# The second layer's modulation as one block behind the first layer's last projection, with early loads

## The reference, cut to what matters

```python
def hybrid_layer(x, c, pos0, k_buf, v_buf, shift_prev, wkv0, conv_buf, h0, lp):
    mod = jax.nn.silu(c) @ lp["w_mod"] + lp["b_mod"]          # (., 3072)
    shift_m, scale_m, gate_m = jnp.split(mod, 3, axis=-1)
    h = rmsnorm(x, lp["norm_pre"]) * (1.0 + scale_m[:, None]) + shift_m[:, None]
    proj = h @ lp["w_in"]                                     # (., 2880)
    qa, ka, va, ga, pb, gb, xc, gc = jnp.split(proj, IN_OFFSETS, axis=-1)
    ...   # A: sliding-window attention, B: RWKV-7 time mixing, C: RG-LRU, each gated
    y = jnp.concatenate([ya, yb, yc], axis=-1) @ lp["w_out"]
    x = x + gate_m[:, None] * rmsnorm(y, lp["norm_post"])
    return x, (k_new, v_new, shift_new, wkv_new, conv_new, h_new)
```

## Time and profile before

| | us |
|---|---|
| three timed runs | 2907.3, 2910.8, 2911.9 |
| the profiled execution, its own time | 2903.7 |
| its span, first to last instruction | 2901.9 |
| TensorE busy in it | 2757.8 (95%) |
| TensorE weight loads | 2016.0 (69%) |
| DVE busy | 1720.0 (59%) |
| ACT busy | 1338.5 (46%) |
| POOL busy | 255.2 (9%) |
| moved by DMA | 119.18 MB |

### The profile page before, as it was taken

The page is one execution under the profiler, slowest core; times in us unless marked ns, Lnnn a source line. Parts: engine busy times, 40 slices in busy tenths (PEclk is TensorE's granted clock), DMA queues, the critical chain, the costliest instruction groups (busy, mean ns, idle before and its releaser), DMA issues.

```text
span 2901.9 us, 63519 instructions
## 1 busy us (share of the span) xinstructions
PE 2757.8 (95%) x25044; PEld 2016.0 (69%) x25044; DVE 1720.0 (59%) x4641; ACT 1338.5 (46%) x3128; POOL 255.2 (9%) x357
## 2 busy tenths in 40 slices
PE   6999999999999999997769999999999999999976
PEld 5777777777777777775457777777777777777753
DVE  1666666666666666665416666665666666666654
ACT  1545444544554444443215544445445554444432
POOL 0010111101101011100001000111011100011000
PEclk8999999999999999999769999999999999999997
DMA  9200000000000000000660000000000000000001
GB/s 341 97 16 24 23 24 23 9 24 24 24 24 17 23 24 23 16 9 22 206 243 16 19 22 23 24 23 17 16 24 24 24 20 21 24 23 16 16 19 33
DMA packets 55176, 119.18 MB, mean 41 GB/s; under 512 B 15312, under 2 KB 27216, under 8 KB 54608
## 3 DMA queue, kind: packets, MB, share of 16 engines
q1 hardware_dynamic: 52912, 114.28, 11.5%
q10 hardware_dynamic: 1952, 0.48, 0.1%
HBM read 96.34 MB, written 18.41 MB: 40 GB/s over the span
## 4 chain that ended last, share of the span: by engine, by line
PE 91%; DVE 4%; DMA 2%; issue 1%; ACT 1%; SPq 0%; POOL 0%; DVEq 0%; POOLq 0%; ACTq 0%
PE G L468 17%; PE G L576 16%; PE M L792 15%; PE G L463 8%; PE M L463 5%; PE M L625 5%; PE M L459 4%; PE M L638 3%; PE G L693 2%; PE G L474 2%; DMA RB<-in_w_mod 2%; PE M L604 1%; PE M L674 1%; PE G L459 1%; DVE Q L1441 1%
## 5 line engine op out<-in xcount | busy, mean ns | idle before, releaser
L468 PEld LDWEIGHTS G<-hT,w_in 128*128 128x128 f32 x4224 | 495.2, 194 | 21.9 <-issue 16.5
L468 PE MATMUL G<-hT,w_in 128*128 128x128 f32 x4224 | 507.1, 278 | 3.3 <-issue 3.3
L576 PE MATMUL G<-hT,w_in 128*128 128x256 f32 (+1 forms) x2048 | 497.1, 385 | 0.0
L792 PE MATMUL M<-w_out,yT 128*128 128x512 f32 x1024 | 452.8, 596 | 5.8 <-DVE yT L1579 5.8
L576 PEld LDWEIGHTS G<-hT,w_in 128*128 128x128 f32 x2048 | 360.4, 189 | 64.7 <-issue 12.3
L792 PEld LDWEIGHTS M<-w_out,yT 128*128 128x128 f32 x1024 | 193.4, 191 | 225.2 <-issue 223.7
L463 PE MATMUL G<-w_in,hT 128*128 128x512 f32 x512 | 244.4, 610 | 0.0
L1441 DVE TENSOR_TENSOR Q<-Q,M 64x256 f32<-64x256 f32 x320 | 133.8, 418 | 130.5 <-PE M L638 127.3
L625 PEld LDWEIGHTS M<-W 64*64 64x64 f32 x4608 | 147.7, 135 | 24.3 <-issue 24.3
L625 PE MATMUL M<-W 64*64 64x64 f32 x4608 | 162.7, 219 | 0.0
L1231 POOL TENSOR_TENSOR RA<-RA,small 128x1024 f32<-128x1024 f32 x32 | 60.6, 1895 | 1136.9 <-DVE small L1493 1136.9
(11 more groups left out here) (413 smaller groups left out, 4562.7 us busy)
## 6 DMA issues: line engine op xcount, KB each, us to landing
w_in<-in_w_in SPq DMA_DIRECT2D x8, 2048.0 KB, 15.1
RA<-in_w_mod SPq DMA_DIRECT2D x16, 512.0 KB, 6.9
W<-in_w_mod SPq DMA_DIRECT2D x16, 512.0 KB, 6.9
xa<-in_x_prompt SPq DMA_DIRECT2D x16, 512.0 KB, 3.7
w_out<-in_w_out SPq DMA_DIRECT2D x2, 4096.0 KB, 18.4
G<-in_x_prompt SPq DMA_DIRECT2D x16, 512.0 KB, 3.5
x_mid<-RA SPq DMA_DIRECT2D x16, 512.0 KB, 2.9
xa<-x_mid SPq DMA_DIRECT2D x16, 512.0 KB, 3.6
```

Of the source, the lines that this page charges most:

```text
L468: last = mm(out[0:width, :], Win[:, k, col:col + width], H[:, k, :], start=k == 0, stop=k == KC - 1)
L576: last = mm(out, Win[:, k, col:col + P], moving, start=k == 0, stop=k == KC - 1)
L792: last = mm(o[:, :], yT[:, k, :], Wout[:, k, 512 * h:512 * h + 512], start=k == 0, stop=k == KC - 1)
```

## The change

- **Start.** SP loads cT first, then chunks of `w_mod`, then two constants, x of tile 0 and 1; ACT takes its silu as soon as cT is there (`c_in`) and loads the other constants itself. The parameters `prm` and `spc` hold both layers, and both layers' softplus chains run behind the first layer's modulation.
- **Second x by another buffer.** Tile 1's x goes to `x2`, which shares `KB` (KR and BK as one tile), and DVE normalises it from there into `xa`.
- **Front.** The gb fill stands ahead of `front`, with its own weight semaphore; on ACT, `decays` comes behind the gb copy.
- **Sample's input early.** The last tile of each layer holds ssq between the two halves of its projection, and DVE's `sample_input()` behind `yB_ready`.
- **Modulation of layer 2.** Its 24 chunks go to six buffers `wnext` that are idle by the end of layer 1's last tile; TensorE computes them as one block behind that tile's projection, into `M0, M1, G0, M2, M0, M1`; ACT copies rows and channels. `modulation(1)` stands in the sample's DVE list.
- **Tile 0 of layer 2** is loaded, normalised and transposed within the end of layer 1's sample.
- **State stores** go out on ACT's queue, after `o_ready` of the last tile. DVE clears the states for layer 2 (`cleared`) behind its first row copy of the sample's projection; it waits for the stores.

The diff, cut to its core:

```diff
+            sp.dma_start(cT[:, :, :], d["cT"]).then_inc(L["c_in"], 16)
             for q in range(NWM - 1):
                 load_w_mod(0, q)
+            sp.dma_start(cst[:, 0:2 * P], d["cst"][:, 0:2 * P]).then_inc(L["const"], 16)
+            sp.dma_start(qk[:, 0:384], d["masks"]).then_inc(L["const"], 16)
...
+        wnext = [flat(xa[:, :]), hT[:, :, 0, :], flat(RA[:, 0:1024]), flat(KB[:, :, :].rearrange("p a b -> p (a b)")),
+                 hT[:, :, 1, :], flat(RB[:, :])]
...
+                def load_next(q):
+                    if q >= NWM:
+                        sp.wait_ge(L["mod_mm"], 24 + (q - NWM + 1))
+                    sp.dma_start(wnext[q % NWM], d["w_mod"][1, q]).then_inc(wmod_in[q % NWM], 16)
...
+                if mixed:
+                    m = NT - 1
+                    sp.wait_ge(s["xT_hi"], DONE(m))
+                    load_next(0)
+                    sp.wait_ge(s["gbc_mm"], DONE(m - 1))
+                    load_next(1)
+                    sp.wait_ge(s["pT1_mm"], DONE(m))
+                    load_next(2)
+                    sp.wait_ge(s["y_mm"], DONE(m))
+                    sp.dma_start(xr, rows(src, m)).then_inc(L["xr_in"], 16)
+                    load_next(3)
+                    sp.wait_ge(s["gbc_mm"], DONE(m))
+                    load_next(4)
+                    sp.wait_ge(s["pv_mm"], DONE(m))
+                    load_next(5)
+                    for q in range(NWM, 24):
+                        load_next(q)
+                    sp.wait_ge(s["o_ready"], DONE(m))
+                    sp.dma_start(rows(dst, m), ob).then_inc(L["y_out"], 16)
+                    sp.wait_ge(L["mod_mm"], 48)
...
+                if mixed:
+                    load_x2(d["x_mid"][P:2 * P, :])
+                    sp.wait_ge(L["modT_mm"], 1 + MODG)
...
+                    sp.wait_ge(smp["dve"], AT("y", l))
+                    sp.dma_start(xa[:, :], d["x_mid"][0:P, :]).then_inc(L["x_in"], 16)
...
                     project(0, M5).then_inc(s["o0_mm"], 1)
                     if ahead:
                         front(n + 1)
+                    else:
+                        pe.wait_ge(smp["dve"], AT("sq", l))
+                        for k in range(KC):
+                            last = mm(M3[:, 0:B], ...)
+                        last.then_inc(smp["pe"], 1)
                     project(1, M4).then_inc(s["o1_mm"], 1)
+                    if fused:
+                        pe.wait_ge(L["padded"], 2)
+                        mod_chunks(0, 1, 2, 3, 4, 5, 6, 7)
+                        mod_fold(0)
+                        pe.wait_ge(s["gbc_out"], DONE(n))
+                        mod_chunks(8, 9, 10, 11)
+                        mod_fold(1)
...
+                        mod_chunks(20, 21, 22, 23)
+                        mod_fold(4)
+                        mod_fold(5)
...
                 for g, (col, width, _) in enumerate(DGROUPS):
+                    if mixed and g == 1:
+                        pe.wait_ge(L["mod_act"], MFOLD[5])
...
+                if mixed:
+                    x_lo((l + 1) * NT)
                 pe.wait_ge(smp["dve"], AT("osq", l))
...
+                if mixed:
+                    x_hi((l + 1) * NT)
...  (ACT)
+                act.wait_ge(s["o_ready"], DONE(l * NT + NT - 1))
+                for out, carry in ((d["k_p"], kT[:, 0:P]), (d["v_p"], Vt[:, 0, :]), (d["shift_p"], pB[:, :, 0]),
+                                   (d["wkv_p"], S[:, 0, :, :]), (d["conv_p"], xcb[:, :, 0:3]), (d["h_p"], hcar[:, :])):
+                    act.dma_start(out[l], carry, ...).then_inc(L["state"], 16)
...  (DVE)
+            def cleared(l):
                 dve.wait_ge(L["state"], l * 96 + 16)
                 ms(pB[:, :, 0:1], 0.0)
...
-                    mask = cst[upper, o:o + 2 * CH].rearrange("p (w c) -> p w c", w=2)
+                    mask = cst[upper, o:o + 3 * CH].rearrange("p (w c) -> p w c", w=3)[:, 0::2]
...
                 for g, (_, width, _) in enumerate(DGROUPS):
                     dve.wait_ge(L["row_mm"], l * (ROWS - MODG) + (g + 1))
-                    cp(rowbuf[g % 2][:, 0:width], (G0, G1)[g % 2][:, 0:width]).then_inc(L["row_out"], 1)
+                    cp(srow[g % 2][:, 0:width], (G1, G0)[g % 2][:, 0:width]).then_inc(L["row_out"], 1)
+                    if mixed and g == 0:
+                        cleared(l + 1)
...
+                if mixed:
+                    dve.wait_ge(L["mod_act"], MFOLD[5])
+                    modulation(l + 1)
```

More of the change, by code:

```diff
@@ L477, in _, with to_channels @@
             for l in range(DEPTH):
-                def to_channels(group, row, out, rows, chunks):
-                    pe.wait_ge(L["row_out"], l * ROWS + (row + 1))
+                def to_channels(buf, row, out, rows, chunks):
+                    pe.wait_ge(L["row_out"], row + 1)
                     for start, width, column in chunks:
-                        last = mm(out[0:width, column:column + rows], rowbuf[group % 2][:, start:start + width],
+                        last = mm(out[0:width, column:column + rows], buf[:, start:start + width],
                                   fold[:, 0:rows], start=True, stop=True)
@@ L774, in tile @@
                         fill_rk(n + 1, Hn)
+                    fused = mixed and not ahead
                     pe.wait_ge(s["yn_ready"], DONE(n))
@@ L827, in _ @@
                 pe.wait_ge(s["o1_mm"], BEFORE((l + 1) * NT))
-                pe.wait_ge(smp["dve"], AT("sq", l))
-                for k in range(KC):
-                    last = mm(M0[:, 0:B], one, dsq[:, k, :], start=k == 0, stop=k == KC - 1)
-                last.then_inc(smp["pe"], 1)
                 pe.wait_ge(smp["dve"], AT("h", l))
@@ L1134, in tile @@
                         low_rank(n + 1)
+                    fused = mixed and not ahead
                     act.wait_ge(s["o0_mm"], DONE(n))
-                    A(RB[:, 0:512], M5[:, :], ACT.Square, accum_out=small[:, 3:4])
+                    A(RB[:, 0:512] if ahead else stB, M5[:, :], ACT.Square, accum_out=small[:, 3:4])
                     if ahead:
                         decays(n + 1)
+                    else:
+                        act.wait_ge(smp["dve"], AT("ms", l))
+                        A(dr2[:, :], dr1[:, :], ACT.Sqrt).then_inc(smp["act"], 1)
@@ L1139, in tile @@
                     act.wait_ge(s["o1_mm"], DONE(n))
-                    A(RB[:, 512:1024], M4[:, :], ACT.Square, accum_out=small[:, 4:5]).then_inc(s["o_squared"], 1)
-                x_square(l * NT, hT[:, :, 1, :])
-                act.wait_ge(L["mod_out"], l + 1)
-                act.wait_ge(L["zeros"], l + 1)
-                h_lo(l * NT, hT[:, :, 0, :])
-                h_hi(l * NT, hT[:, :, 0, :])
-                for step in (copy_rk, copy_wka, copy_v, low_rank, decays):
+                    A(RB[:, 512:1024] if ahead else qk[:, 0:512], M4[:, :], ACT.Square, accum_out=small[:, 4:5]).then_inc(s["o_squared"], 1)
@@ new lines, in tile @@
+                    if fused:
+                        mod_row(0)
+                        mod_row(1)
+                        mod_copy(0)
+                        mod_row(2)
+                        mod_copy(1)
+                        mod_row(3)
+                        mod_copy(2)
+                        mod_row(4)
+                        mod_copy(3)
+                        mod_row(5)
+                        mod_copy(4)
+                        mod_copy(5)
+                if l == 0:
+                    x_square(0, hT[:, :, 1, :], 0)
+                    act.wait_ge(L["mod_out"], 1)
+                    act.wait_ge(L["zeros"], 1)
+                    h_lo(0, hT[:, :, 0, :])
+                    h_hi(0, hT[:, :, 0, :])
+                    for k in range(DEPTH):
+                        act.wait_ge(L["sp1"], k + 1)
+                        A(spc[:, k, 1, :], spc[:, k, 0, :], ACT.Exp, scale=-1.0).then_inc(L["sp2"], 1)
+                        act.wait_ge(L["sp1"], k + 1)
+                        act.wait_ge(L["sp3"], 2 * k + 1)
+                        A(spc[:, k, 5, :], spc[:, k, 2, :], ACT.Ln).then_inc(L["sp2"], 1)
@@ L1330, in _, with x_mean, modulation @@
-                tt(gpc[:, :, :], mod[:, 16:24, :], over(par("npost"), 2, 9), ALU.mult).then_inc(L["gpc"], 1)
+            def x_mean(m, src=xa[:, :]):
+                dve.wait_ge(s["x_root"], DONE(m))
+                ts(xa[:, :], src, small[:, 7:8], ROOT_D, ALU.mult, ALU.mult).then_inc(s["xn_ready"], 1)
+            def modulation(l):
+                ll(tt(mod[:, :, :], (modr[:, :, :] if l else M0[:, 0:216].rearrange("p (q b) -> p q b", q=24)),
+                      over(par(l, "bmod"), 2, 9), ALU.add))
+                ll(ts(gs[:, :, :], mod[:, 8:16, :], 1.0, None, ALU.add))
+                tt(gs[:, :, :], gs[:, :, :], over(par(l, "npre"), 2, 9), ALU.mult).then_inc(L["mod_out"], 1)
@@ L1356, in token_shift @@
                     dve.wait_ge(s["y_mm"], BEFORE(m))
[L1357 removed]
```

(5 more changed lines are left out.)

384 lines of the change are left out of this document (220 added, 164 removed).

## The result

| | us, median (lowest to highest, runs) | ratio to before, 95% interval |
|---|---|---|
| before | 2909.05 (2903.54 to 2911.91, 4) | |
| after | 2886.32 (2884.14 to 2889.56, 4) | 0.9925 [0.9906, 0.9944] |
| after, taken again later | 2886.29 (2876.86 to 2889.05, 6) | 0.9926 [0.9912, 0.9940] |
| forecast | 2870.6, range 2856 to 2884 | |

The change makes the kernel faster, but by 22.7 us where 40.2 were forecast; the median lies 2.3 us above the upper end of the range. The direction was right, the size was not.

What follows compares the result with a forecast made beforehand. The prediction took TensorE to bound the kernel (91% of the chain), with DMA full at the start and between the layers. Gains 5.0 + 4.0 + 22.8 + 8.4 = 40.2 took 2910.8 to 2870.6 us, range 2856 to 2884.

Steps and rivals of the forecast that it cites:

- Between the layers, 22.8: From layer 1's last projection to layer 2's r,k fill: 62.4 us removed, 39.6 added, gain 22.8 us.
- A new wait: DVE's clearing waits for layer 1's six state stores, delaying TensorE's fold 1: +6.1 us, ends -2 and +12.
- rival B: State stores' completions wait for SP's 2.2 MB of loads across queues: 5.8 us more, 2876.4 us; chance 0.17.
- The block of 24 chunks: Layer 2's modulation behind layer 1's last projection: 30.4 us added, ends 25 and 38.
- The r,k fill comes behind a busy TensorE: Layer 2's first fill runs at full clock instead of half: -1.0 us of added time, ends 0 and -2.6.
- `modulation(1)`, 0.85: Three ops in the middle of the sample's DVE chain, between the layers: 0.85 us added.
- Start, 5.0: Program start: chunk 0 of w_mod goes out 5.9 us earlier; gain 5.0 us, ends 3 and 8.3.
- Fronts, 4.0: Front of each layer: gb fill covers TensorE's wait for xs; gain 2.0 us a layer, ends 1 and 4.7.
- Tail, 8.4: Layer 2's tail: sample input made during the projection, fold 0 earlier; gain 8.4 us, ends 6 and 9.1.
- Edits at nothing: KR and BK in one tile, `par(l, ...)`, one semaphore less, strided Gram-copy mask: 0 us, ends -1.5 and +3.
- Rival C: The 32 tiles pay for the strided mask and DVE products, slower than before: 2914.8 us; chance 0.04.
- rival D: The early start does nothing as TensorE waits inside the projection; some 16 us lost, 2887 us; chance 0.04.

Runs made afterwards that it cites:

- experiment 3: Changed kernel with SP's loads of the sample's caches, x row 1 and wkv state held until layer 1's six state stores landed: 2881.62 us, ratio 0.9916.
- experiment 4: Changed kernel with the shift state first copied by ACT into contiguous columns, so its store reads 128 pieces of 28 bytes: 2879.81 us, ratio 0.9908.
- experiment 6: Changed kernel with modulation chunks 7, 10, 13, 16, 19 and 22 sent to two contiguous idle buffers instead of hT's halves: 2882.52 us, ratio 0.9922.
- Experiment 10: Changed kernel with five extra useless 128x512 matmuls, four in TensorE's attention-step waits, one behind x row 0's last transposes: 2879.64 us, ratio 0.9913.
- experiment 8: Changed kernel with the old front order: low-rank matmuls ahead of the gb fill, decays ahead of the gb copy: 2888.76 us, ratio 0.9944.
- experiment 12: The combined kernel with nine extra useless 128x512 matmuls in TensorE's waits, at the start, mid-kernel and layer 2's tail: 2857.95 us, ratio 0.9830.
- experiment 5: Changed kernel with the shift state packed and layer 1's state stores issued inside the modulation block: 2873.01 us, ratio 0.9887.
- the combined kernel: Changed kernel with late zeroing, packed shift state, contiguous late chunks, two x loads behind w_in's first piece: 2864.18 us, ratio 0.9856; again 2864.65 us, 0.9860.

## Why the forecast was wrong, step by step

**Between the layers, 22.8: the step that failed.** Two of its terms carry nearly all.

- *"A new wait", +6.1.* Mechanism, place and the instruction it holds were right; the size was not: 14.8 in the mean of seven profiles (range 11.5 to 19.4, the first being the longest). "With 8.6 the last lands at 1417" took h_p's landing from a stretch where the stores shared a queue with SP's loads, and I read it as a property of the last store. The stores' own 10 us begin with the 3.5 KB of the shift state (9.1 us alone, experiment 3; 6.2 packed, with the loads beside it, experiment 4). In the same list of the kernel before it stood at 8.0 us beside 2.5 for k_p, and I didn't look at it; but v_p stood at 8.1 there, so that the list alone would not have named it. On top of them come 3 to 8 us, 4.7 in the mean, for SP's loads in the same microseconds. That is rival B, with a price of 5.8 us. And "from fold 1 to the last copy of projected columns is 10.3" was taken from a warm TensorE; behind a wait of 13.6 us it took 15.1. The end of +12 that I gave this term did not hold it.
- *"The block of 24 chunks", 30.4.* It took 35.1 and 36.2. "17 more at the pace of the second modulation before" carried over a pace without asking into what the chunks are written: the new buffers include hT, in pieces of 512 bytes (experiment 6). With contiguous ones it takes 30.6. The latency of chunk 6 (3.7), and the six resident chunks (one every 0.44 us) were no worse than forecast (1374.3 and 3.7 make 1378.0, not the 1378.3 written there). The end of the block was: 4.5 us from the last chunk, cold, where 2.5 were put.
- *"The r,k fill comes behind a busy TensorE", -1.0.* It took 10.28 us, more than the 9.84 before. TensorE is not busy in the sample's steps; it waits for DVE. Experiment 10 shows that the clock was the reason (granted 0.71 in that fill, 1.00 with the extra matmuls), and that it can be had.
- `modulation(1)`, 0.85: the stage from the last copy to xsT grew by 1.8, of which 1.2 in the w_out groups (6.16 us for two, cold; 5.3 when warm).

**Start, 5.0.** 3.0 in the first profile, 4.4 in the mean of eleven (50.3 to 53.2 for the same code). Right, by the mean; this stage's own scatter, 2.9 us, is over half of its term.

**Fronts, 4.0.** 1.9, by experiment 8. The mechanism was right, hole and all; the price of the cold clock behind the hole was put too low.

**Tail, 8.4.** 5.9. Fold 0 came 7.7 us earlier; 1.7 went back in the one group behind a wait of 2.5 us, which the forecast had not costed and experiment 12 takes away. The other 0.7 is in fold 0 itself.

**Edits at nothing.** Right: from q fill to last projection the layers take 1258.62 and 1258.63 before, 1259.06 and 1258.61 after. Rival C and rival D are out. (The loops hold 28 tiles, 14 a layer, and not the 30 of the forecast; no term used it.)

With the wait and the block at their measured means (8.7 and 5.2 us more) the forecast would have been 2884.5. What else was missed is 2.2 us in the fronts, 2.5 in the tail and 1.0 at the fill. A cold clock behind a wait stands in all three places (granted 0.50, 0.51 and 0.71). Taking it away was tried at the fill (experiment 10) and for 1.7 us of the tail (experiment 12); for the fronts it is read from the rows of experiment 8 alone. Together the three are more than the 1.8 left to the median, and single profiles differ from one another and from a median by as much. Open stays what the last 4 us of experiment 5 are, and why h_p's landing scatters from 13.1 to 18.3 us in the same code.

## What to carry to other kernels

A wait on a batch of stores costs what the slowest of them takes, and here that went by the count of its pieces, not by its bytes: look at each row of the issue list and at how each source lies in memory, not at the last row. The clearing of a buffer belongs just ahead of its next use, not at the first free moment of an engine on the path. A pace measured with one set of destination buffers is no forecast for another; and a term taken from a warm TensorE has to be priced cold when a wait is put before it (here the waits were of 2.5, 4.9 and 13.6 us). A wait made shorter may give back less than its length, for the same reason (experiment 4).

## What the runs showed of the hardware

- A store of 3.5 KB in 896 pieces of 4 bytes took 9.1 us where 64 KB took 1.6, and each of the three stores issued behind it in its queue took 10.1 to 10.5. On another queue, beside a stream of 512 KB loads, the same pieces made the stage of the stream 6.3 us longer (63.5 against 57.2 with the packed store, one profile each). The Trainium skill, "DMA: Bandwidth & Descriptors", section "Queues, rings and completion order", has each DMA engine take turns between queues by packets, which fits both; no run here shows the turns themselves.
- Loads in pieces of 512 bytes, a third of the stream, cost it 11% of its rate (291 against 327 GB/s).
- Five matmuls without a use, some 5 us of work put in waits, raised the granted clock of the following fill from 0.71 to 1.00 and made the kernel 4 to 7 us faster; the same five in the combined kernel raised it to 0.88 only. Two at the start, in a stretch at half clock, gave a shorter fill (7.5 us instead of 9.0 and 9.2) but no gain that the time shows.
- Behind a wait of 4.5 us of TensorE the granted clock was 0.51 for the next 16 us of work without a pause (experiment 4); behind one of 8.7 us it was back at 1.00 after 5.6 us (experiment 10). A longer wait did not mean a longer cold stretch.
